# A fused transformer block: the first attention in 32 units of two maps, with projection panels between them

## The reference

```python
h = rms_norm(x, attn_pre_g)
q_a, k_a, v_a, q_b, k_b, v_b = split(h @ w_in)          # 2304 columns = 18 tiles of 128
y_a = rms_norm(swa_sink_attention(q_a, k_a, v_a))       # 8 heads of 64, 2 kv heads, window 128, ALiBi, sink
y_b = diff_attention(q_b, k_b, v_b)                     # 4 heads: softmax(map 0) - lam * softmax(map 1), values 128 wide
x = x + rms_norm(concat(y_a, y_b) @ w_out)              # 1024 x 1024
x = x + rms_norm(conv_ffn(rms_norm(x)))                 # 1024 -> 2*4096 -> 1024
# second block: latent attention with top-k choice and a gated linear recurrence, in parallel:
mixed = sigmoid(m_a) * y_attn + sigmoid(m_r) * y_rnn
out = rms_norm(x + mixed @ w_out_2)
```

## Time and profile before

| | |
|---|---|
| median of 3 runs | 1437.79 us (1436.31 to 1441.23) |
| profiled execution | 1440.45 us, its span 1438.7 us |
| PE busy | 1353.6 us, 94% of the span, mean granted clock 0.968 |
| DVE, ACT, POOL busy | 852.3, 587.6, 230.4 us |
| input projection | 13.7 to 103 us |
| first attention, to the first pass of `out1` | 103.1 to 230.2 us |
| `out1` | 230.2 to 274.2 us |
| second attention | 1161.9 to 1301.8 us |

### The profile page before, as it was taken

The page is one execution under the profiler, slowest core; times in us unless marked ns, Lnnn a source line. Parts: engine busy times, 40 slices in busy tenths (PEclk is TensorE's granted clock), DMA queues, the critical chain, the costliest instruction groups (busy, mean ns, idle before and its releaser), DMA issues.

```text
span 1438.7 us, 16244 instructions
## 1 busy us (share of the span) xinstructions
PE 1353.6 (94%) x6038; PEld 1055.6 (73%) x6038; DVE 852.3 (59%) x1410; ACT 587.6 (41%) x859; POOL 230.4 (16%) x185
## 2 busy tenths in 40 slices
PE   7998878999999999999999989999799989999996
PEld 6886436768888888888888767777577855557885
DVE  5118672488888558846873251569998156663242
ACT  5116574353443223423331343333465345554231
POOL 2440011100000000000000323411003421114451
PEclk9998978999999999999999999899999999999998
DMA  5320000212223223223222222402113210001421
GB/s 185 117 88 30 1 30 15 102 37 110 88 90 114 87 88 115 89 87 106 99 87 101 94 99 87 147 30 88 58 60 107 98 59 30 30 30 59 150 85 58
DMA packets 17784, 116.46 MB, mean 81 GB/s; under 512 B 1984, under 2 KB 2240, under 8 KB 4544
## 3 DMA queue, kind: packets, MB, share of 16 engines
q1 hardware_dynamic: 16320, 108.35, 21.4%
q10 hardware_dynamic: 1408, 7.37, 1.3%
HBM read 111.52 MB, written 4.19 MB: 80 GB/s over the span
## 4 chain that ended last, share of the span: by engine, by line
PE 78%; DVE 15%; ACT 4%; issue 2%; DMA 0%; POOL 0%; ACTq 0%; DVEq 0%; SPq 0%
PE PG L337 22%; PE PG L338 21%; PE PG L339 21%; PE PX L624 3%; PE PX L475 2%; PE PG L653 2%; PE PX L663 1%; DVE MD L1495 1%; DVE XC L1521 1%; DVE MD L1513 1%; PE PX L373 1%; DVE WL L1135 1%; DVE SM L1510 1%; DVE XT L1365 1%; PE PX L640 1%
## 5 line engine op out<-in xcount | busy, mean ns | idle before, releaser
L337 PE MATMUL PG<-XH,WH 128*128 128x512 f32 x1136 | 448.7, 395 | 17.2 <-DVE WL L1135 9.8
L338 PE MATMUL PG<-XL,WH 128*128 128x512 f32 x1136 | 443.6, 390 | 0.0
L339 PE MATMUL PG<-XH,WL 128*128 128x512 f32 x1136 | 443.2, 390 | 0.0
L317 POOL TENSOR_TENSOR WL<-RAW,WH 128x512 fp32r<-128x512 f32 x168 | 225.8, 1376 | 1175.7 <-ACT WH L711 1175.7
L711 ACT ACTIVATE WH<-RAW 128x2048 fp32r<-128x2048 f32 x100 | 191.6, 1916 | 452.4 <-PE PG L339 446.8
L337 PEld LDWEIGHTS PG<-XH,WH 128*128 128x128 f32 x1136 | 214.0, 188 | 70.8 <-DVE WL L1135 12.7
L338 PEld LDWEIGHTS PG<-XL,WH 128*128 128x128 f32 x1136 | 214.2, 189 | 45.3 <-issue 1.7
L339 PEld LDWEIGHTS PG<-XH,WL 128*128 128x128 f32 x1136 | 214.1, 188 | 45.0
L1135 DVE TENSOR_TENSOR WL<-RAW,WH 128x2048 fp32r<-128x2048 f32 x58 | 132.7, 2288 | 19.2 <-ACT WH L711 19.0
L337 PE MATMUL PG<-AH,WH 128*128 128x512 f32 x256 | 99.6, 389 | 0.0
L338 PE MATMUL PG<-AL,WH 128*128 128x512 f32 x256 | 99.6, 389 | 0.0
(11 more groups left out here) (278 smaller groups left out, 1799.0 us busy)
## 6 DMA issues: line engine op xcount, KB each, us to landing
RAW<-panels SPq DMA_DIRECT2D x100, 1024.0 KB, 4.7
x_spill<-XT ACTq DMA_DIRECT2D x1, 2048.0 KB, 6.3
XT<-x_spill ACTq DMA_DIRECT2D x1, 2048.0 KB, 7.7
outT<-SQ SPq DMA_DIRECT2D x4, 512.0 KB, 3.0
XT<-xT ACTq DMA_DIRECT2D x2, 512.0 KB, 6.8
XT<-xT SPq DMA_DIRECT2D x2, 512.0 KB, 9.4
RGW<-rgw ACTq DMA_DIRECT2D x1, 1024.0 KB, 5.0
UK<-uk ACTq DMA_DIRECT2D x1, 512.0 KB, 5.9
```

What stands on the lines that cost most here:

```text
L317: ins = pool.tensor_tensor(WL[:, s].rearrange("p a b -> p (a b)")[:, piece], RAW[:, s, piece], WH[:, s].rearrange("p a b -> p (a b)")[:, p ...
L337: pe.matmul(o, WH[:, s, c, ms], xh[:, c, :], start=(c == 0), stop=False)
L338: pe.matmul(o, WH[:, s, c, ms], xl[:, c, :], start=False, stop=False)
L339: mm = pe.matmul(o, WL[:, s, c, ms], xh[:, c, :], start=False, stop=(c == DC - 1))
```

## The change

`in1` has three panels now, six more are `fill1`, and `out1`'s four panels hold the matrix in quarters: 512 inner rows by 512 columns each, inner half first. Local and differential attention share one pipeline of 32 units `w`: 16 with a pair of local heads (one in each kv group) and one query block, 16 with a differential head and one block. Behind units 0 to 23 stand two `fill_piece`s of six passes each, behind units 25 to 31 and the end two `low_piece`s, which multiply the first four mix tiles (the local heads) with the first two quarters; the last two quarters follow after the units and DVE adds the two halves. The sink is put as a 257th (129th) column in the buffer of logits, ahead of the exponential; ALiBi slopes come in through a scale on the queries and `scale=-slope` in the fused logits operation. `factor` loads its first table ahead of its wait, except for n2, n4, n6. In the second block sigmoid is written with tanh.

```diff
-STAGES = [("in1", 8), ("in1v", 1), ("out1", 4), ...
+STAGES = [("in1", 3), ("fill1", 6), ("out1", 4), ...
+FILL_TILES = [(6, 10), (14, 15), (7, 11), (16, 17), (8, 12), (9, 13)]
 # PE
+            def fill_piece(n):
+                k, piece = divmod(n, 8)
+                m, quarter = divmod(piece, 4)
+                p = FIRST["fill1"][0] + k
...
+                if piece == 0:
+                    pe.wait_ge(w_lo, p + 1)
+                    if k >= 1:
+                        pe.wait_ge(evac, p)
+                elif piece == 4:
+                    pe.wait_ge(once("fill1_out"), k + 1)
+                for c in (2 * quarter, 2 * quarter + 1):
...
+            def low_piece(n):
+                t, half = divmod(n, 2)
+                p = FIRST["out1"][0] + t // 4
+                if half == 0:
+                    if t % 4 == 0:
+                        pe.wait_ge(w_lo, p + 1)
+                        pe.wait_ge(evac, p)
                     else:
+                        pe.wait_ge(once("low_out"), t - t // 4)
+                for c in (2 * half, 2 * half + 1):
+                    if t == 0:
+                        pe.wait_ge(once("mix_split"), c + 1)
+                    mm = out_pass(PX[:, 2, :], p, t % 4, c, 0)
...
+            for w in range(32):
+                if w + 2 < 16:
+                    swa_scores(w + 2)
+                elif w + 2 < 32:
+                    diff_scores(w + 2)
+                att_turn(w)
+                if w % NB == 0 and w >= NB:
+                    swa_pv(w // NB - 1) if w <= 16 else diff_pv(w // NB - 5)
...
+                if w < 24:
+                    fill_piece(2 * w)
+                    fill_piece(2 * w + 1)
+                elif w >= 25:
+                    low_piece(2 * (w - 25))
+                    low_piece(2 * (w - 25) + 1)
+                if w >= 18 and w % NB == 2:
+                    mix_sums((w - 18) // NB)
+            diff_pv(3)
+            low_piece(14)
+            low_piece(15)
+            mix_sums(4)
...
+            p = FIRST["out1"][0] + 3
+            pe.wait_ge(w_lo, p + 1)
+            for t in range(4):
...
+                if t == 3:
+                    pe.wait_ge(evac, p)
+                    pe.wait_ge(acc, 1)
+                    pe.matmul(PX[:, 1, :], O1024[:], SQY[:, 0, :], start=True, stop=False)
+                    pe.matmul(PX[:, 1, :], O1024[:], SQY[:, 1, :], start=False, stop=False)
+                o = PX[:, (0, 2, 3)[t], :] if t < 3 else PG[:, 0, :]
+                for c in range(4, DC):
+                    mm = out_pass(o, p, t, c, 4)
 # ACT
             def factor(name, dst, bank=1, count=1):
+                if name not in ("n2", "n4", "n6"):
+                    act.preload_act_table_set("natural_log")
...
+            for w in range(32):
+                if w + 1 < 32:
+                    att_exp(w + 1)
+                att_copy(w)
+                if w in (9, 10, 16, 17):
+                    copy_values({9: 1, 10: 2, 16: 3, 17: 4}[w], 1)
+                if w % NB == 0 and 4 <= w <= 24:
+                    hi_ahead(FIRST["fill1"][0] + w // NB - 1)
+                if w == 24:
                     mix_hi(0)
+                if w >= 17 and w % NB == 1:
+                    mix_square((w - 17) // NB)
+                if w >= 18 and w % NB == 3:
+                    factor("mix", MR[:], 1, (w - 19) // NB + 1)
+                if w >= 25 and w % NB == 1:
+                    mix_hi((w - 21) // NB)
+                if w == 29:
+                    hi_ahead(FIRST["out1"][0])
             mix_hi(3)
             mix_square(4)
             factor("mix", MR[:], 1, 5)
             mix_hi(4)
+            hi_ahead(FIRST["out1"][0] + 1)
+            hi_ahead(FIRST["out1"][0] + 2)
 # DVE
+                for m in range(2):
...
+                    dve.tensor_tensor_reduce(out=PD[s][:, m, 0:n], in0=dist, in1=PG[:, 2 * (w % 2) + m, 0:n],
+                                             scale=-slope, scalar=first, op0=ALU.add, op1=ALU.min,
+                                             accum_out=NM3[:, 2 * s + m:2 * s + m + 1]).then_inc(once("att_logits"), 1)
...
+            for w in range(32):
+                if 2 <= w <= 24 and w % 2 == 0:
+                    fill1_out((w - 2) // 4, 0 if w % 4 == 2 else 1)
+                if w >= 26:
+                    low_out(w - 26)
+                if w + 2 < 32:
+                    att_logits(w + 2)
+                if w + 1 < 32:
+                    att_probs(w + 1)
+                if w % NB == 1 and w >= 5:
+                    swa_out(w // NB - 1) if w <= 17 else diff_out(w // NB - 5)
+                if w >= 20 and w % NB == 0:
+                    mix_scale((w - 20) // NB)
+                if w == 24:
                     mix_lo(0)
+                if w >= 25 and w % NB == 1:
+                    mix_lo((w - 21) // NB)
...
+            for t in range(4):
+                if t < 3:
+                    dve.wait_ge(once("y1_tile"), t + 1)
+                else:
+                    add_pairs("n2", SQY, 2)
+                    dve.wait_ge(panel_done, p + 2)
+                dve.tensor_tensor(Y1[:, 4 + t, :], PX[:, (0, 2, 3)[t], :] if t < 3 else PG[:, 0, :], PROJ[:, 14 + t, :], ALU.add)\
+                    .then_inc(once("y1_out") if t < 3 else evac, 1)
```

More of the change, by code:

```diff
@@ L298, in _ @@
             pool.wait_ge(consts, 6)
[L300 to L304, removed]
+            pool.affine_select(out=PD[1][:, 0, 0:256], in_=EC[:, 2 * P:], compare_op=ALU.is_ge, fill=FAR,
+                               base=-1, pattern=[[1, 256]], channel_multiplier=-1).then_inc(consts, 1)
             pool.memset(O512[:], 1.0 / 512).then_inc(consts, 1)
@@ new lines, in diff_scores @@
+            def diff_scores(w):
+                h, qb = divmod(w - 16, NB)
+                if qb == 0:
+                    pe.wait_ge(evac, FIRST["fill1"][0] + (1, 3, 5, 6)[h])
+                pe.wait_ge(once("att_logits"), 2 * w - 2)
+                n = (qb + 1) * P
+                for m in range(2):
+                    rows = slice(m * HD, (m + 1) * HD)
+                    mm = pe.matmul(PG[:, 2 * (w % 2) + m, 0:n], PROJ[rows, 6 + h, qb * P:(qb + 1) * P],
+                                   PROJ[rows, 10 + h, 0:n], start=True, stop=True)
+                mm.then_inc(once("att_s"), 1)
@@ new lines, in mix_sums @@
+            def mix_sums(k):
+                tiles = range(4) if k == 0 else [3 + k]
+                if k == 0:
+                    pe.wait_ge(consts, 9)
+                    pe.wait_ge(once("v_copied"), 5)
+                else:
+                    pe.wait_ge(once("mix_r"), k)
+                for c in tiles:
+                    pe.wait_ge(once("mix_sq"), c + 1)
+                    mm = pe.matmul(PX[:, 1, :], O512[:] if k == 0 else O128[:], MSQ[:, c, :], start=(c == tiles[0]),
+                                   stop=(c == tiles[-1]))
+                mm.then_inc(once("mix_sum"), 1)
@@ L449, in swa_pv, with diff_pv @@
+            def diff_pv(h):
+                pe.wait_ge(once("att_copied"), 16 + NB * h + NB)
+                if h == 0:
+                    pe.wait_ge(once("swa_out"), 4)
+                else:
+                    pe.wait_ge(once("diff_out"), h)
+                for kb in range(NB):
+                    mm = pe.matmul(PX[:, 3, kb * P:], VB[:, h, kb, :], PTD[:, h % 2, kb, kb * P:],
                                    start=(kb == 0), stop=(kb == NB - 1), skip_group_check=True)
[L450 removed]
@@ L469, in unit_turn @@
+            for t in range(2):
+                pe.wait_ge(sq, 4 + t)
+                mm = pe.matmul(PX[:, 1, :], O1024[:], SQY[:, 6 + t, :], start=False, stop=(t == 1))
+            mm.then_inc(once("n2_sum"), 1)
+            keep_warm(30)
             def unit_turn(pre, src, u, qb, maps):
@@ L491, in _ @@
[L491 to L510, removed]
@@ L780, in _ @@
             factor("n1", R[:])
-            hi_stage("in1")
+            for p in range(3):
+                hi_ahead(p)
             def copy_values(t, bank):
@@ L1731, with quarters @@
     w_out = np.concatenate([a["w_out"][:512][perm], a["w_out"][512:]], 0)
+    order = [0, 1, 2, 3, 4, 5] + [t for pair in FILL_TILES for t in pair]
+    w_in = np.concatenate([w_in[:, 128 * t:128 * t + 128] for t in order], 1)
+    def quarters(w):
+        return np.stack([w[512 * k:512 * k + 512, 512 * n:512 * n + 512].reshape(4, 128, 512).transpose(1, 0, 2).reshape(128, 2048)
+                         for k in range(2) for n in range(2)])
     up = a["w_up"].reshape(1024, 2, 32, 128).transpose(0, 2, 1, 3).reshape(1024, 8192)
```

465 lines of the change are left out of this document (211 added, 254 removed).

## The result

| | before | changed |
|---|---|---|
| median (lowest to highest) | 1439.1 us of 4 runs (1436.31 to 1441.23) | 1416.26 us of 4 runs (1416.14 to 1418.66) |
| profiled execution, its span | 1440.45, 1438.7 us | 1418.66, 1416.4 us |
| PE busy, mean granted clock | 1353.6 us, 0.968 | 1338.6 us, 0.971 |

The ratio is 0.9846 (interval 0.9825 to 0.9868). Forecast were 1415 us and, for the profiled execution, 1417.3.

A forecast was written before the change was run, and what follows sets the result against it. One queue of TensorE work bounds the kernel; gains of 19.5 up to E, 2.3 behind E and 1.3 elsewhere sum to 23.1 us: 1440.45 to 1417.3 profiled, 1415 median; own range 1405 to 1424, with (a) and (b) 1396 to 1431.

The forecast's parts named there:

- rival (d): The 32 units: the passes fill no idle time but are added to each unit's chain; 1438 us, chance 0.06.
- E: Instant when the output projection's last pass ends: 274.15 us before, forecast 254.6, so 19.5 us earlier.
- The opening: Before the first transpose: it comes at 56.9 us, 6.74 after the first scores (ends 3 and 8); clock loses 2.6.
- TensorE's work: The 32 units' scores, transposes, products, norm sums and projection passes: 152.5 us, 150.9 without what lies in the opening.
- What waits inside: TensorE's waits in the 32 units: 8.3 us at units 25 and 26, 2.8 at 30, 3.2 clock, 1 GpSimd; 15.3 total.
- rival (c): GpSimd's low parts hold VectorE and idle TensorE at each of eight panels: 3.7 us each, 30 in all; 1444, chance 0.06.
- The tail: Rest of the output projection after the units: 23.9 us, plus 5.0 for wait and clock before the last tile.
- Behind E: Next factor ready 6.2 us after E instead of 9.3; less 0.8 for the clock, net 2.3 saved (0 to 4).
- Elsewhere: Tanh for Sigmoid removes a table load before the second attention's exponentials: 1.3 us, ends 0 and 3; other changes nothing.
- (a): Waits are covered because tiles are split earlier: 15.3 + 5.0 falls to some 2, 18 us more; 1397, chance 0.23.
- (b): ScalarE paces the differential half: four mix factors of 3.9 us ahead of exponentials show, 15.6 more; 1430, chance 0.15.

The follow-up runs named there:

- the opening's experiment: Changed kernel with ScalarE's third high part behind the copy of unit 1 and first exponentials ahead of the value copy: 1409.19 us, 0.9792 of the kernel before.
- The combined version: Changed kernel with pair sums behind the last tile, unit 24's mix high parts first, later opening high part, and mix_lo(1) one unit later: 1399.43 us.
- the order: Changed kernel with ScalarE making the first four mix tiles' high parts ahead of the panel's in unit 24: 1413.36 us, 0.9817 of the kernel before.
- sigmoid experiment: Changed kernel with Sigmoid and old multiplications restored at both gates and norm factors' table loads back behind their waits: 1417.2 us, 0.9844 of the kernel before.
- the scalings in unit 21: Changed kernel with VectorE's first four mix scalings moved from unit 20 to unit 21: 1417.03 us, 0.9854 of the kernel before.
- no input panels between the units: Changed kernel with all 48 fill_pieces run before the first scores, units 0 to 23 carrying no passes: 1439.68 us, 1.0007 of the kernel before.
- the low part later: Changed kernel with VectorE's mix_lo of a differential head one unit later: 1416.9 us, 0.984 of the kernel before.
- no half output projection between the units: Changed kernel with the loop's fourteen low_pieces all moved behind the units: 1433.45 us, 0.9956 of the kernel before.

## Why the prediction was right, point by point

- **The mechanism** (TensorE's work is the bound, filling closes its gaps) is shown: take the filling out and the time is the old one, and also with the artefacts of the two experiments set aside some 15 and 10 us of it are filling; rival (d) is false. The change of form, units of two maps with the new tail, is worth at most the 9 us named there; the estimate in the section on the result gives it 3 to 4. One sign that I named did not come: TensorE is busy for 90% at 0.93 from 50 us to E, not for over 93% near 0.95.
- **The opening**: first transpose forecast 56.9, at 55.63; 2.6 us of clock, and by the rows about 2.7 (4.37 x 0.45 + 6.00 x 0.12). Right, and its main cause (GpSimd beside VectorE, 2.1 of the 2.8 us that can be taken away) is shown by the opening's experiment: there the first transpose comes 3.0 us behind the first scores, the lower end of the term, and here 5.8.
- **TensorE's work**: units 0 to 23 forecast from the second attention's prices; unit 24 began at 172.09, about 2 us later than these give. Four waits stand there that I hadn't priced, 0.30 and 0.65 at 137.73 and 138.93, 1.56 and 0.65 at 161.54 and 162.74, and 1.6 us of clock behind the last (6.00 x 0.27): 4.8 in all. The second pair is GpSimd's low part (154.21, 6.40 us) beside the first four scalings, 4.79 us for four. All the work of the 32 units took 149.7 us (227.2 less 58.3 for the opening and less the 19.2 of the next point), where I had 150.9. (A slip that changes nothing: 43.95 over four is 10.99 and not 10.93.)
- **What waits inside**: sizes off in both directions. Units 25 and 26: five waits of 0.68, 0.31, 0.27, 2.21 and one of 2.1 before, 5.6 in all where I had 8.3; unit 30: 2.49 + 1.17 where I had 2.8. The clock was the term mis-sized. I gave 1.6 us to each place: behind units 25 and 26 it was 5.2 (5.06 x 0.42 + 3.52 x 0.50 + 6.00 x 0.22), behind unit 30 nothing. Waits and clock together 19.2 against 15.3 (3.2 + 1.6 + 5.6 + 5.2 + 3.7); with the opening done 1.2 us sooner and 1.2 less of work, the units ended at 227.2 and not 225.7.
- **GpSimd, rival (c)**: the low parts at 76.67, 94.01 and 112.22 held TensorE nowhere. Those at 50.56, 154.21 and 177.03 did, and two more a little: at 132.14 two 384-column steps of VectorE took 0.96 and 1.52 us instead of 0.42 and 0.62, ahead of the waits of 0.30 and 0.65; at 213.36 two 512-column steps took 1.00 and 1.64 instead of 0.49 and 0.75, ahead of the 1.17. It was no cost per panel but one per coincidence with VectorE's dearest steps. In place of my 1 us for all this the four unpriced waits take 3.2 and the clock 1.6.
- **The tail**: late low part forecast 1.2, measured 0.17; wait before the last tile forecast 3.4, measured 3.27 and at the place named; the clock behind it forecast 1.6, measured 2.9 (last tile and sums 7.42 us instead of 4.56, which the opening experiment took for them at full clock; the 3.8 in my expectations counted one sum instead of two). The two sums take 1.8, and I had 0.9. E at 257.5, forecast 254.6.
- **Behind E**: factor forecast 6.2 us behind E, measured 5.9 (257.53 to 263.43); the next projection started 11.25 behind E, before 14.66: 3.4 gained where I had 2.3.
- **Elsewhere**: the 1.3 for Tanh is false: at its place nothing moved (6.74 us with and without the table load). The distance does grow from 20.0 at 269 us to 22.3 at the end, but by scatter. Behind the first pass of the next projection the trace before takes 1149.9 us, the changed kernel's 1147.6, and the eleven other traces of kernels that don't differ there 1146.3 to 1149.5. Most of that lies in the second attention, where the clock falls behind the same waits in one execution and not in another: from 40 to 60 us behind its first scores TensorE has 17.9 us of work, at 0.91 in the trace before and at 1.00 in the changed kernel's. So 2.3 us came where I had 1.3 for a wrong reason; that is luck, and it made up for part of the tail's error.
- **Rivals (a) and (b)**: (a) forecast 1397 for waits that are covered. The changed kernel doesn't cover them. The combined version is at 1399.4, but that is another sum: some 5 us of it lie in the opening, which (a) leaves as it is, and waits of 2.42 and 2.49 are still there. (b) is not seen: no wait in the list above is released by ScalarE's exponentials. One goes back to them by a step, the 1.17: VectorE waited 1.92 us for exponentials which ScalarE started at 213.19, behind a panel's high part (211.39) and not behind a mix factor.

## What to carry to other kernels

Filling an engine's idle stretches with a neighbouring stage's independent work pays by idle time and by the slow clock behind it, by the estimate above in about equal parts here; to find out, run the same pieces unfilled, in front of the loop, and subtract what the hand-overs of that version cost. A wait of TensorE of three us or more cost up to nearly twice its length here (3.27 and 2.9 of clock); take those away first. The cause of a gain is found by comparing stretches between fixed points of the traces: a whole trace carries some 3 us of scatter from elsewhere. A single wait inside a ring of three engines is only worth removing if what would be late next is on time: of three such moves two gave nothing.

## What the runs showed of the hardware that I had not expected

- The same wait doesn't always cost the same. Before the last tile TensorE waited for 3.26 or 3.27 us in nine traces of kernels that don't differ there. In four of them (the changed kernel's two, the order and the sigmoid experiment) the first two products took 2.05 and 1.91 us, at half clock; in three (the opening, the scalings in unit 21, no input panels between the units) they ran at once at full clock; in the other two (the low part later, no half output projection between the units) only part of the stretch was slow, and sums and last tile took 6.2 and 6.3 us. The opening experiment's tail:

```profile
241.76 1.10 PE L579 MATMUL PX<-SQY,O 128*128 128x512 f32 x2 [3.26 <-DVE SQY L1174]
...
246.32 1.02 PE L587 MATMUL PX<-SQY,O 128*128 128x512 f32 x2
```

  4.56 us from first to last, beside 7.42 in the changed kernel. So 2.9 us hang on something that isn't the wait's length; what decides it no run here shows, and a change elsewhere can win or lose them. In unit 22 it is the same: the waits of 1.56 and 0.65 stand in ten traces; in eight the clock was at 0.79 in the 8 us behind them, in two (the opening, the first combined version) at 1.00. The opening's wait of 3.64 was followed by a lower clock in every trace that has it, for 1.5 to 2.8 us of loss. Behind 2.49 and 1.17 us at 212 to 218 the clock stayed at 1.00.
- GpSimd's subtractions (1.25 us each, 5.02 for four at 76.67) also grow when both work: 6.40 and 6.33 beside VectorE's runs of two-input operations, which took 1.2 and 1.6 us each (4.79 and 6.41 for four) instead of 0.68 and 0.62 (2.73 and 2.49).
